# S5 preparation in a two-block network: coefficient chain on GpSimd, table operations in blocks of at most 512 columns

## What is computed

```python
h = h + 0.5 * swiglu(rms_norm(h, ffn_norm[0, 0]), w_gate, w_up, w_down)   # stage ffn0, width 2816
hn = rms_norm(h, mix_norm[0])                                             # then s5_mixer(hn, ...)

# in s5_mixer; a_re, a_im: 64 groups x 64 states, log_dt: 64
dt = jnp.exp(log_dt)[:, None]
mag = jnp.exp(a_re * dt)
lam_re = mag * jnp.cos(a_im * dt)
lam_im = mag * jnp.sin(a_im * dt)
den = a_re * a_re + a_im * a_im
num_re = lam_re - 1.0
coef_re = (num_re * a_re + lam_im * a_im) / den
coef_im = (lam_im * a_re - num_re * a_im) / den
bb_re, bb_im = cmul(coef_re[..., None], coef_im[..., None], b_re, b_im)
# bu = u x bb; st = associative scan over time with lam; y = st_re x c_re - st_im x c_im
```

## Time and profile before

| | |
|---|---|
| median of 3 runs | 1741.67 us (1741.25 to 1742.12) |
| the profiled execution | 1747.93 us, span 1746.0 us |
| TensorE busy | 1647.4 us, 94% |
| VectorE busy | 1086.2 us, 62% |
| ScalarE busy | 759.3 us, 43% |
| GpSimd busy | 454.7 us, 26% |
| mean granted TensorE clock | 0.963 of full speed |

### The profile page before, as it was taken

The page is one execution under the profiler, slowest core; times in us unless marked ns, Lnnn a source line. Parts: engine busy times, 40 slices in busy tenths (PEclk is TensorE's granted clock), DMA queues, the critical chain, the costliest instruction groups (busy, mean ns, idle before and its releaser), DMA issues.

```text
span 1746.0 us, 31473 instructions
## 1 busy us (share of the span) xinstructions
PE 1647.4 (94%) x13068; PEld 1578.1 (90%) x13068; DVE 1086.2 (62%) x1067; ACT 759.3 (43%) x995; POOL 454.7 (26%) x413
## 2 busy tenths in 40 slices
PE   5989998799999999999899999889999998999997
PEld 5979997599999999999789999785999996699997
DVE  7797669866555665564466555545655565475555
ACT  5324350154433543446454343545533345643332
POOL 6999317610000100017430000535100013510000
PEclk8989996799999999999999999989999997999999
DMA  6534540045554455544425555350455542045552
GB/s 223 191 142 168 195 147 1 1 169 180 181 189 173 159 204 189 181 171 146 145 99 186 187 181 189 125 181 1 145 193 189 174 166 97 25 164 186 180 192 72
DMA packets 39012, 265.74 MB, mean 152 GB/s; under 512 B 4352, under 2 KB 6400, under 8 KB 7328
## 3 DMA queue, kind: packets, MB, share of 16 engines
q1 hardware_dynamic: 37808, 261.41, 43.1%
q0 software_dynamic: 1136, 3.38, 0.7%
HBM read 263.70 MB, written 1.06 MB: 152 GB/s over the span
## 4 chain that ended last, share of the span: by engine, by line
PE 80%; DVE 11%; POOL 5%; issue 2%; ACT 2%; DMA 0%; DVEq 0%; SPq 0%; POOLq 0%; ACTq 0%
PE ps L533 74%; DVE gst L1449 2%; PE ps L823 2%; PE ps L813 2%; POOL tsq L278 2%; DVE wlo L1269 1%; DVE xlo L1275 1%; PE ps L801 1%; DVE tk L1499 1%; POOL trr L371 1%; DVE h L1285 1%; DVE t L1423 1%; DVE t L1424 1%; DMA h<-in_xT 0%; ACT pm L1186 0%
## 5 line engine op out<-in xcount | busy, mean ns | idle before, releaser
L1269 DVE TENSOR_TENSOR wlo<-raw,whi 128x2048 fp32r<-128x2048 f32 x246 | 597.1, 2431 | 268.6 <-ACT whi L963 268.2
L533 PE MATMUL ps<-xhi,whi 128*128 128x256 f32 x2048 | 585.8, 286 | 28.7 <-DVE wlo L1269 16.3
L963 ACT CAST whi<-raw 128x2048 fp32r<-128x2048 f32 x246 | 467.7, 1904 | 269.6 <-PE ps L533 269.5
L533 PE MATMUL ps<-xlo,whi 128*128 128x256 f32 x2048 | 582.8, 285 | 0.0
L533 PE MATMUL ps<-xhi,wlo 128*128 128x256 f32 x2048 | 582.6, 284 | 0.0
L533 PEld LDWEIGHTS ps<-xhi,whi 128*128 128x128 f32 x2048 | 396.7, 194 | 33.4 <-DVE wlo L1269 17.5
L533 PEld LDWEIGHTS ps<-xlo,whi 128*128 128x128 f32 x2048 | 396.8, 194 | 0.1
L533 PEld LDWEIGHTS ps<-xhi,wlo 128*128 128x128 f32 x2048 | 396.5, 194 | 0.0
L533 PE MATMUL ps<-hhi,whi 128*128 128x256 f32 x1216 | 344.4, 283 | 0.0
L533 PE MATMUL ps<-hhi,wlo 128*128 128x256 f32 x1216 | 344.1, 283 | 0.0
L533 PE MATMUL ps<-hlo,whi 128*128 128x256 f32 x1216 | 344.1, 283 | 0.0
(11 more groups left out here) (235 smaller groups left out, 2066.7 us busy)
## 6 DMA issues: line engine op xcount, KB each, us to landing
raw<-in_wstream SPq DMA_DIRECT2D x247, 1024.0 KB, 4.9
h<-in_xT SPq DMA_DIRECT2D x1, 1024.0 KB, 8.1
out_hT<-h SPq DMA_DIRECT2D x2, 512.0 KB, 3.0
biasA<-bias_rows POOLq DMA_DIRECT2D x5, 192.0 KB, 3.7
biasB<-bias_rows POOLq DMA_DIRECT2D x3, 192.0 KB, 4.1
braw<-in_s5b POOLq DMA_DIRECT2D x1, 512.0 KB, 3.9
CL<-in_s5c POOLq DMA_DIRECT2D x4, 128.0 KB, 4.4
tg<-in_tgain POOLq DMA_DIRECT2D x1, 384.0 KB, 3.5
```

The source lines that it names most:

```text
L533: return pe.matmul(o, l, r, start=first, stop=last, skip_group_check=True)
L963: act.copy(whi[:, slot, :], raw[:, slot, :]).then_inc(S("whi_ready"), 1)
L1269: dve.tensor_tensor(wlo[:, slot, :], raw[:, slot, :], whi[:, slot, :], ALU.subtract)\
```

## The change

The coefficient chain moves from VectorE to GpSimd, where it stands between the loads of C and the tables. Three kinds of instruction change with it: two fused multiply-adds become a multiply and an add each, and the reciprocal of `den` becomes a power with the exponent -1. On ScalarE, the exponent for `dt` moves ahead of the first `xhi`; the rest of `s5_angles` moves into ffn0, behind the first `hidden` and ahead of the loop. The semaphore `s5_coefs` goes. The memsets of `LB` and `CL` and the table operations are cut so that none has over 512 columns a partition (the memsets 1024): `tile_blocks(w)` gives blocks of 512 // w rows, rounded down to a power of two. So w = 32 has two blocks, w = 63 four, `times_lambda` and the change of sign two; below that all stays one block. The operations on B have 512 columns before and after.

```diff
+            def tile_blocks(w):
+
+                n = max(1, min(NP_S5, 512 // w)) if w else NP_S5
+                n = 1 << (n.bit_length() - 1)
+                return [slice(q, q + n) for q in range(0, NP_S5, n)] if w else []
+
+            def s5_coefficients():
...
+                pool.wait_ge(S("par_loaded"), 16)
+                pool.wait_ge(S("s5_dt"), 1)
+                TT_(Q["x"], a_re, Q["dt"], ALU.mult).then_inc(S("s5_x"), 1)
+                chain(TT_(Q["th"], a_im, Q["dt"], ALU.mult))
+                chain(TS(Q["k"], Q["th"], 1 / (2 * np.pi), big, ALU.mult, ALU.add))
+                chain(TS(Q["k"], Q["k"], big, None, ALU.subtract))
+                chain(TS(Q["tA"], Q["k"], -turn_hi, None, ALU.mult))
+                chain(TT_(Q["r"], Q["th"], Q["tA"], ALU.add))
+                chain(TS(Q["tA"], Q["k"], -turn_lo, None, ALU.mult))
+                chain(TT_(Q["r"], Q["r"], Q["tA"], ALU.add))
+                TS(Q["r"], Q["r"], PI, -PI, ALU.min, ALU.max).then_inc(S("s5_red"), 1)
+                chain(TT_(Q["tA"], a_re, a_re, ALU.mult))
+                chain(TT_(Q["tB"], a_im, a_im, ALU.mult))
+                chain(TT_(Q["den"], Q["tA"], Q["tB"], ALU.add))
+                chain(TT_(Q["den"], Q["den"], power[:, 1:2].to_broadcast([P, NP_S5]), ALU.pow))
+                pool.wait_ge(S("s5_sin"), 2)
...
-            chain(pool.memset(LB[:, :, :, :, :], 0.0))
-            chain(pool.memset(CL[:, :, :, :, :], 0.0))
+            for r in range(2):
+                for i in range(2):
+                    chain(pool.memset(LB[:, r, i], 0.0))
+                    chain(pool.memset(CL[:, r, i], 0.0))
...
-            pool.wait_ge(S("s5_coefs"), 1)
+            s5_coefficients()
...
-                if w > 0:
-                    cm = Ec[:, :, m:m + 1].to_broadcast([P, NP_S5, w])
+                for qs in tile_blocks(w):
+                    nq = qs.stop - qs.start
+                    cm = Ec[:, qs, m:m + 1].to_broadcast([P, nq, w])
...
             def times_lambda(dst_re, dst_im, re, im, op_re, op_im):
-                for dst, x, y, op in ((dst_re, re, im, op_re), (dst_im, im, re, op_im)):
-                    chain(pool.tensor_tensor(dst, x, lr, ALU.mult))
...
+                for qs in tile_blocks(32):
...
+                    for dst, x, y, op in ((dst_re, re, im, op_re), (dst_im, im, re, op_im)):
+                        chain(pool.tensor_tensor(dst[:, qs], x[:, qs], lr, ALU.mult))
...
-            chain(pool.tensor_scalar(CL[:, 1, 0], CL[:, 1, 0], -1.0, None, ALU.mult))
+            for qs in tile_blocks(32):
+                chain(pool.tensor_scalar(CL[:, 1, 0, qs], CL[:, 1, 0, qs], -1.0, None, ALU.mult))
...
                 silu(st, 0, None)
                 hidden(st, 0, None, 0, 2, None)
+                if st == "ffn0":
+                    s5_angles()
                 with act.Fori(0, (FFN_IT - 1) // 2) as i:
...
             def s5_angles():
 
-                act.wait_ge(S("par_loaded"), 16)
-                act.activation(Q["dt"], log_dt, ACT.Exp).then_inc(S("s5_dt"), 1)
                 act.wait_ge(S("s5_x"), 1)
...
+            act.wait_ge(S("par_loaded"), 16)
+            act.activation(Q["dt"], log_dt, ACT.Exp).then_inc(S("s5_dt"), 1)
             x_high(0)
             split_hi(1)
-            s5_angles()
             ffn("ffn0")
...
             split_lo(1)
-            s5_coefficients()
             ffn("ffn0")
```

More of the change, by code:

```diff
@@ L399, in normalise, with TT_, TS @@
                         .then_inc(S(st + "_pn"), 1)
+            def tile_blocks(w):
[3 more added lines that the diff above has]
+            def s5_coefficients():
+                def TT_(o, x, y, op):
+                    return pool.tensor_tensor(o, x, y, op)
+                def TS(o, x, p, q, op0, op1=None):
+                    return pool.tensor_scalar(o, x, p, q, op0, op1) if op1 is not None else pool.tensor_scalar(o, x, p, q, op0)
+                big = 1.5 * 2.0 ** 23
+                turn_hi = 6.28125
+                turn_lo = 2 * np.pi - turn_hi
+                pool.wait_ge(S("par_loaded"), 16)
[14 more added lines that the diff above has]
+                pool.wait_ge(S("s5_sin"), 2)
+                chain(TT_(Q["c"], Q["sh"], Q["sh"], ALU.mult))
+                chain(TS(Q["c"], Q["c"], -2.0, 1.0, ALU.mult, ALU.add))
+                chain(TT_(Q["lr"], Q["mag"], Q["c"], ALU.mult))
+                chain(TT_(Q["li"], Q["mag"], Q["s"], ALU.mult))
+                chain(TS(Q["nr"], Q["lr"], 1.0, None, ALU.subtract))
+                for o, p, q, op in (("cr", Q["nr"], Q["li"], ALU.add), ("ci", Q["li"], Q["nr"], ALU.subtract)):
+                    chain(TT_(Q["tA"], p, a_re, ALU.mult))
+                    chain(TT_(Q["tB"], q, a_im, ALU.mult))
+                    chain(TT_(Q["tA"], Q["tA"], Q["tB"], op))
+                    chain(TT_(Q[o], Q["tA"], Q["den"], ALU.mult))
+                chain(TT_(Q["mag2"], Q["mag"], Q["mag"], ALU.mult))
+                chain(TT_(Q["tA"], Q["s"], Q["s"], ALU.mult))
+                chain(TS(Q["e2c"], Q["tA"], -2.0, 1.0, ALU.mult, ALU.add))
+                chain(TT_(Q["tB"], Q["s"], Q["c"], ALU.mult))
+                chain(TS(Q["e2s"], Q["tB"], 2.0, None, ALU.mult))
@@ L425, in _ @@
                 w = min(m, NC - 1 - m)
-                if w > 0:
-                    cm = Ec[:, :, m:m + 1].to_broadcast([P, NP_S5, w])
[L428 to L431, removed]
+                for qs in tile_blocks(w):
+                    nq = qs.stop - qs.start
+                    cm = Ec[:, qs, m:m + 1].to_broadcast([P, nq, w])
+                    smm = Es[:, qs, m:m + 1].to_broadcast([P, nq, w])
+                    cj, sj = Ec[:, qs, 1:1 + w], Es[:, qs, 1:1 + w]
+                    co, so = Ec[:, qs, m + 1:m + 1 + w], Es[:, qs, m + 1:m + 1 + w]
+                    tmp = etmp[:, qs, 0:w]
                     chain(pool.tensor_tensor(co, cm, cj, ALU.mult))
@@ L450, in _ @@
                     chain(pool.tensor_tensor(o, o, btmp[rows], op))
-            lr = Q["lr"].unsqueeze(2).to_broadcast([P, NP_S5, 32])
-            li = Q["li"].unsqueeze(2).to_broadcast([P, NP_S5, 32])
-            tmp = etmp[:, :, 0:32]
             def times_lambda(dst_re, dst_im, re, im, op_re, op_im):
-                for dst, x, y, op in ((dst_re, re, im, op_re), (dst_im, im, re, op_im)):
-                    chain(pool.tensor_tensor(dst, x, lr, ALU.mult))
-                    chain(pool.tensor_tensor(tmp, y, li, ALU.mult))
-                    chain(pool.tensor_tensor(dst, dst, tmp, op))
+                for qs in tile_blocks(32):
+                    nq = qs.stop - qs.start
+                    lr = Q["lr"][:, qs].unsqueeze(2).to_broadcast([P, nq, 32])
+                    li = Q["li"][:, qs].unsqueeze(2).to_broadcast([P, nq, 32])
+                    tmp = etmp[:, qs, 0:32]
+                    for dst, x, y, op in ((dst_re, re, im, op_re), (dst_im, im, re, op_im)):
+                        chain(pool.tensor_tensor(dst[:, qs], x[:, qs], lr, ALU.mult))
+                        chain(pool.tensor_tensor(tmp, y[:, qs], li, ALU.mult))
+                        chain(pool.tensor_tensor(dst[:, qs], dst[:, qs], tmp, op))
             times_lambda(LB[:, 0, 0], LB[:, 1, 0], LB[:, 0, 1], LB[:, 1, 1], ALU.subtract, ALU.add)
             pool.wait_ge(S("c_loaded"), 64)
-            chain(pool.tensor_scalar(CL[:, 1, 0], CL[:, 1, 0], -1.0, None, ALU.mult))
+            for qs in tile_blocks(32):
+                chain(pool.tensor_scalar(CL[:, 1, 0, qs], CL[:, 1, 0, qs], -1.0, None, ALU.mult))
             times_lambda(CL[:, 0, 1], CL[:, 1, 1], CL[:, 0, 0], CL[:, 1, 0], ALU.add, ALU.subtract)
@@ L1365, in out_projection @@
                         before=lambda b: split_lo(F + b + 2))
[L1367 to L1403, removed]
```

## The result

The changed kernel takes 1748.33 us (median of 7 runs, 1747.51 to 1750.17) against 1742.12 of the kernel before (1741.04 to 1745.97): a ratio of 1.003, 95% interval 1.0017 to 1.0042. The forecast was 1745.5 us with 1737 to 1752 as its range and "slower" as the likeliest sign. So the change costs 0.2 to 0.3%, near the limit of what these runs can tell.

The account below looks back on a forecast made before the run. TensorE with two holes bounds the kernel; after the change GpSimd's preparation, ending at 231.8 us against TensorE's asking at about 224, decides. Later stage +1.8 and clock +2.0 give +3.8 on 1741.67: 1745.5 us, range 1737 to 1752.

Parts of the forecast that it names:

- (a): GpSimd's start: eight memsets, 0.3 us and four DMA issues, done at 31.2 us.
- (b): Coefficient chain on GpSimd: 30 operations, 10.5 us, and a power on 32 columns, 5.4 us; together 16.0 us.
- rival C: The power on GpSimd takes twice the line, 10.8 us: +9 us, 1751; chance 0.12.
- (d): Cutting of GpSimd's table operations: 37 more pieces at 0.29 us each, 10.8 us.
- (e): More stalls of GpSimd beside VectorE before S5: 71.8 us where 55 were, 16.7 more.
- (f): `norm_scale(1)` on GpSimd behind the preparation: 5.8 us, to 237.6; the stage after it begins 1.8 us later.
- (g): Slow TensorE clock at the start of S5 after idling: 2.0 us, with ends 0 and 2.6.
- Rival A: At the start of S5 the clock comes back for proj: +1.8 us, 1743.5, no difference; chance 0.14.
- second hole: In ffn0 TensorE waits 8.55 us for a `wlo`, until 121.04; forecast to go, 10.6 us with the clock.
- first hole: In ffn0 TensorE idles 7.53 us until 34.25; a new one of some 5.5 us replaces it, only 2 gained.
- Rival B: GpSimd's preparation is done by about 220 us, so not last: -10 us, 1731.8; chance 0.12.
- Rival D: Cutting does nothing for VectorE in ffn0; TensorE asks at 235 us, time hardly differs; part of the forecast.

Follow-up runs that it names:

- e3: Changed kernel without its second `times_lambda` (12 GpSimd operations; that part of the computation left out): 1734.14 us, ratio 0.994.
- e4: Changed kernel with further clears of K0 on GpSimd just ahead of `s5_prepared`, about 5 us more: 1752.07 us.
- e5: Changed kernel with the second `times_lambda` moved behind `norm_scale(1)`, with its own semaphore, all computed: 1732.97 us, ratio 0.9919.
- e8: Changed kernel once more, no edit, beside the kernel before on the same chip: 1747.77 us against 1745.94, ratio 1.0016.
- e7: Changed kernel with matmuls nobody reads, 44 ahead of the wait for `s5_prepared` and 26 ahead of `stats`: 1747.20 us.
- e0: Kernel before once more, no edit, for a second profile: 1744.99 us.
- e9: Kernel before with only the last doubling (w = 63) cut, into four blocks of 8 rows: 1736.62 us, ratio 0.9953.
- e2: Changed kernel with nothing cut, so only the coefficient chain moved to GpSimd: 1740.54 us, ratio 0.9969.
- e1: Kernel before with only the memsets and table operations cut, coefficient chain left on VectorE: 1733.98 us, ratio 0.9938.
- e6: e5 with GpSimd's clears ahead of `norm_scale(0)`, B and C loads behind `s5_red`, `s5_angles` ahead of the first norm's root: 1728.73 us, ratio 0.9894.

## Why the prediction was right, and by what luck

**The mechanism** was as forecast and is shown: GpSimd, not TensorE, sets the start of S5. TensorE asks at 228.21 - 5.53 = 222.7 us (forecast 224) and is idle until `s5_prepared`; e3, e4 and e5 move GpSimd's end and little else, and the time follows.

**The sum for GpSimd**, term by term. (a) The start: 31.34 against 31.2. (b) The power: 5.46 against 5.4, so rival C falls. (d) was not measured alone; 504 columns at 1.05 and 1.28 us are on the lines used. (e) was 3.7 too much: GpSimd was busy 19.75 + 166.30 = 186.1 us; less 96.5 for the tables, 13.5 for the chain and 7.8 for cutting (37 x 0.29 without the gaps of 0.08), as forecast and not measured one by one, that leaves 68 for stalls and not 71.8. A hindered operation lost 1.93 us in the rows above rather than 1.97, and `wlo` 4, which fell beside the power, cost only the 0.55 by which the next operation waited. So the end came at 228.1 and not 231.8. (f) 5.4 us for the norm, 5.8 forecast.

**The stage behind it** began at 233.59 in this profile, 2.2 us sooner than before where I had 1.8 later; e8 has 234.59. (g) The clock then took more than the 2.0 set down for it, and more than its upper end of 2.6: the 50 matmuls 9.13 us against 6.18, 2.95. By profiles the whole is +0.7 us at S5 in one and +1.8 in the other, not +3.8. Rival A (the clock comes back) has happened in e4, whose 50 matmuls took 6.45 us, and is made to happen in e7.

**The base** was the step that failed without harm. I added the difference worked out against one profile to the median of the runs, as if that profile were one of them with a constant on top. It was not: by e0, the second hole is 8.55 us in one execution and 5.88 in another, the clock behind the first hole differs by 1.4 us, and that profile, at 1747.9, was longer than all of the first seven runs. The changed kernel's profile (1749.2) was near its median (1748.3). So the difference of the medians in the first comparison is 6.2 us (base 1742.1), and in e8 it is 1.8. At the S5 mark the two profiles of the changed kernel are 0.7 and 1.8 us behind that of before, and 4.4 and 5.5 behind e0's. The forecast of 3.8 lies between: against the profile that it was worked out from, the sum was 2 to 3 us too high, and the base error, up to 5.5 us, had the other sign. That the forecast came so near is luck. Why the kernel before is near 1742 more often in one set of runs than in another I can't say. It was so in the first seven runs alone: e0 to e7 ran on one chip, e8 and e9 on another, and the medians of before are 1746.6, 1747.2 and 1745.9 there; of these 63 runs 11 are longer than that profile.

**The first hole** was forecast at 5.5 us and is 4.49. ScalarE loads four tables, not three: exponent, sine, one ahead of `whi` 4 and one more for SiLU at 42.25, which delays nothing. `wlo` 4 is through at 42.8, sooner than the 43 to 44 said. **The second hole** went as forecast; e9 shows that w = 63 was all of it. Rival B (GpSimd is not last) was wrong here and is what e5 makes of it: its -10 us came as -14 by the runs and -16 by the S5 mark. Rival D did not arise.

## What to carry to other kernels

Work that is moved onto an engine with slack spends that slack once for each part: here 16 us of chain, some 11 of cutting and 13 of stalls (by the sum; by e2 and e1, 19 for the chain and 25 for cutting, each with its stalls and each alone) together put GpSimd's end 39 us later while TensorE's question came 11 us sooner, and 45 us of slack that neither part alone used up were gone. Before moving work, add up the receiving engine's time to the point where its result is asked for, with the stalls that it takes from its neighbour, and look whether everything ahead of that point has to be there; what is only needed later goes behind it (e5). And a base can scatter by itself by more than the difference sought, here 8 us and more against 2 to 6: take the median of many runs for a difference of 0.2%, and don't add a difference between profiles to a median.

## What the runs showed of the hardware that I had not expected

**A long GpSimd power doesn't hold VectorE back.** I had it from the Trainium skill (SBUF — State Buffer, Who interferes with whom) that whoever issues first has the shared ports for the whole instruction and the other is blocked. In the changed kernel the `wlo` at 40.47 begins within the power from 36.52 to 41.98 and takes its usual 2.29 us, and in e6 (GpSimd, then VectorE) one lies wholly inside, with the power 0.4 us longer than elsewhere:

```profile
32.94 5.82 POOL L410 TENSOR_TENSOR sm<-sm,power 128x32 f32<-128x32 f32 x1
38.84 2.28 POOL L410 TENSOR_TENSOR sm<-sm 128x32 f32<-128x32 f32 x1
```

```profile
35.93 2.29 DVE L1323 TENSOR_TENSOR wlo<-raw,whi 128x2048 fp32r<-128x2048 f32 x1 [1.11 <-ACT whi L1016]
```

Multiplies and additions of 504 to 2016 columns did hold `wlo` back until their end: the longest took 3.4 us beside those of 504 and 512 and 6.5 beside those of 2016. The measurement decides: for this power on 32 columns the rule doesn't hold. Why is not shown.

**The granted clock comes back at different times behind like waits.** The same 50 matmuls behind 16 transposes and 1.73 us of idle took 9.13, 9.19 and 6.45 us in three executions, the shortest behind the longest wait. It is the same behind the holes: the mean granted clock of the first 10 us behind a hole of 7.5 or 7.6 us was 0.69, 0.86 and 0.76 (before, e0, e9), behind one of 4.5 us 0.72 and 0.83 (the changed kernel and e8). That is up to 1.4 us between like executions, as much as some of the effects looked for here. No run here tells what decides it.
